# High weights times both halves of the rows in one matmul, in the stages of 256 tokens of a 6-layer transformer

## The reference

```python
def first_block(x, ...):                # 256 tokens
    for i in range(2):                  # i = 0: dilated attention, i = 1: mLSTM
        h = h + mixer(rms_norm(h), w_in, w_out)
        h = h + swiglu(rms_norm(h), ffn_w_in[i], ffn_w_out[i])

def swiglu(xn, w_in, w_out):            # D_FF = 2816
    gu = xn @ w_in
    return (jax.nn.silu(gu[..., :D_FF]) * gu[..., D_FF:]) @ w_out

def second_block(x, c, ctx, ...):       # 256 tokens, and 256 of context up to the last layer
    for i in range(4):                  # neighbourhood attention, conformer, short conv, attention
        x = x + mod_l[:, 2] * y_l
        m_l = modulate(rmsnorm(x, norm2_g[i]), mod_l[:, 3], mod_l[:, 4])
        x = x + mod_l[:, 5] * sq_relu_mlp(m_l, mlp_w1[i], mlp_w2[i])
        # the same for ctx while a later layer needs it

def sq_relu_mlp(h, w1, w2):             # 1024 -> 4096 -> 1024
    return jnp.square(jax.nn.relu(h @ w1)) @ w2
```

## Time and profile before

| | us |
|---|---|
| median of 3 runs | 2985.64 |
| lowest, highest | 2983.21, 2987.95 |
| span of the profiled execution | 2983.2 |
| TensorE busy in it | 2888.3 (97%) |
| TensorE's weight loads busy | 2524.0 (85%) |
| VectorE busy | 2004.9 (67%) |
| ScalarE busy | 1202.5 (40%) |
| GpSimd busy | 349.9 (12%) |

### The profile page before, as it was taken

How to read it: one execution, slowest core, us unless ns; L and a number is a source line. 1 busy time by engine, 2 the same in 40 slices (tenths; PEclk the granted TensorE clock), 3 DMA queues, 4 the chain that set the end, 5 groups by cost and what they waited for, 6 DMA issues and landing times.

```text
span 2983.2 us, 43523 instructions
## 1 busy us (share of the span) xinstructions
PE 2888.3 (97%) x18080; PEld 2524.0 (85%) x18080; DVE 2004.9 (67%) x3284; ACT 1202.5 (40%) x1993; POOL 349.9 (12%) x542
## 2 busy tenths in 40 slices
PE   7999999989999999999999999999999999998998
PEld 7999998889997778888866888888888888877898
DVE  7776887668655557777745677777777777554665
ACT  5444544554444444223314533223243222443543
POOL 0000001000022220000131100011010000243000
PEclk9999999999999999999999999999999999999999
DMA  7544675347655424555473255553535555465453
GB/s 241 168 159 152 216 229 190 120 161 234 204 125 81 72 64 147 157 167 169 132 190 107 80 168 163 169 165 124 170 120 164 168 163 169 117 96 86 142 184 128
DMA packets 362277, 451.85 MB, mean 151 GB/s; under 512 B 12656, under 2 KB 332432, under 8 KB 362080
## 3 DMA queue, kind: packets, MB, share of 16 engines
q1 hardware_dynamic: 326976, 329.83, 34.1%
q0 software_dynamic: 34944, 118.65, 16.9%
q10 hardware_dynamic: 160, 0.59, 0.1%
HBM read 438.60 MB, written 1.05 MB: 147 GB/s over the span
## 4 chain that ended last, share of the span: by engine, by line
PE 79%; DVE 12%; ACT 5%; DMA 2%; issue 1%; POOL 1%; DVEq 0%; SPq 0%; ACTq 0%
PE ps L1352 23%; PE ps L1354 23%; PE ps L1353 23%; DVE lo L1932 4%; PE ps L1530 1%; ACT hi L1602 1%; PE ps L1373 1%; PE ps L1517 1%; DVE NB L1963 1%; DMA NB<-in_na_rpb 1%; PE ps L1375 1%; PE ps L1374 1%; DVE MX L2008 1%; PE ps L1505 1%; DVE XN L1969 1%
## 5 line engine op out<-in xcount | busy, mean ns | idle before, releaser
L1352 PE MATMUL ps<-XN,hi 128*128 128x256 f32 (+1 forms) x3184 | 1048.8, 329 | 32.9 <-DVE XN L1949 9.9
L1353 PE MATMUL ps<-XN,hi 128*128 128x256 f32 (+1 forms) x3184 | 1029.9, 323 | 0.0
L1354 PE MATMUL ps<-XN,lo 128*128 128x256 f32 (+1 forms) x3184 | 1029.6, 323 | 0.0
L1932 DVE TENSOR_TENSOR lo<-raw,hi 128x1024 fp32r<-128x1024 f32 (+1 forms) x626 | 739.2, 1221 | 250.6 <-ACT hi L1602 245.4
L1602 ACT ACTIVATE hi<-raw 128x1024 fp32r<-128x1024 f32 (+1 forms) x626 | 620.6, 1040 | 443.5 <-PE ps L1354 440.7
L1352 PEld LDWEIGHTS ps<-XN,hi 128*128 128x128 f32 x3184 | 610.6, 192 | 106.6 <-issue 17.4
L1354 PEld LDWEIGHTS ps<-XN,lo 128*128 128x128 f32 x3184 | 610.8, 192 | 46.1
L1353 PEld LDWEIGHTS ps<-XN,hi 128*128 128x128 f32 x3184 | 611.2, 192 | 44.8
L2008 DVE CUSTOM_DVE_ANT_0 MX<-MW,C 128x1024 bf16<-128x1024 f32 x384 | 477.2, 1243 | 130.7 <-DMA MW<-in_mod_w 123.8
L1352 PE MATMUL ps<-H,hi 128*128 128x512 f32 (+1 forms) x1072 | 380.2, 355 | 0.0
L1353 PE MATMUL ps<-H,hi 128*128 128x512 f32 (+1 forms) x1072 | 379.7, 354 | 0.0
(11 more groups left out here) (255 smaller groups left out, 3194.8 us busy)
## 6 DMA issues: line engine op xcount, KB each, us to landing
raw<-in_mlp_w SPq DMA_DIRECT2D x128, 1024.0 KB, 5.3
MW<-in_mod_w POOLq DMA_DIRECT2D x192, 512.0 KB, 3.8
raw<-in_ffn_w_in SPq DMA_DIRECT2D x44, 1024.0 KB, 5.4
raw<-in_attn_w_in SPq DMA_DIRECT2D x36, 1024.0 KB, 4.9
raw<-in_na_wqkv SPq DMA_DIRECT2D x24, 1024.0 KB, 5.0
raw<-in_ffn_w_out SPq DMA_DIRECT2D x16, 1024.0 KB, 5.1
raw<-in_mlstm_w_in SPq DMA_DIRECT2D x12, 1024.0 KB, 5.1
raw<-in_cv_w SPq DMA_DIRECT2D x12, 1024.0 KB, 6.2
```

What stands on the lines that cost most here:

```text
L1352: e.matmul(out, whi, xhi, start=first, stop=False)
L1353: e.matmul(out, whi, xlo, start=False, stop=False)
L1354: i = e.matmul(out, wlo, xhi, start=False, stop=last)
L1932: e.tensor_tensor(lo[:, a:b], raw[:, a:b], hi[:, a:b].bitcast(F32), ALU.subtract).then_inc(*low.says(("lo", j, i), ("spent", j) if i else ...
```

## The change

A stage of 256 tokens fills half of a bank of 512 columns. With `pair`, one matmul of 512 columns takes the high weights against both halves of the rows: the hi half goes to columns 0 to 255, the lo half to 256 to 511. The matmul of the low weights against the high half adds to columns 0 to 255. The result is the sum of both halves of the bank, and the reader forms it. Pairing is on in attention q and k, the output projections of attention, mLSTM and the last layer, feed-forward down, and the last MLP. Feed-forward up, v projections, and everything of 512 tokens stay.

```diff
@@ TensorE
-    def product(j, t, k, kt, bank, x, first, last, whole=True, final=True):
+    def product(j, t, k, kt, bank, x, first, last, whole=True, final=True, pair=False):
...
-        e.matmul(out, whi, xhi, start=first, stop=False)
-        e.matmul(out, whi, xlo, start=False, stop=False)
-        i = e.matmul(out, wlo, xhi, start=False, stop=last)
+        if pair:
+            e.matmul(m.ps[b][:, :].rearrange("p (h n) -> p h n", h=2), whi, both_of(m, x, k), start=first, stop=False,
+                     skip_group_check=True)
+        else:
+            e.matmul(out, whi, xhi, start=first, stop=False)
+            e.matmul(out, whi, xlo, start=False, stop=False)
+        i = e.matmul(out, wlo, xhi, start=False, stop=last, skip_group_check=pair)
@@ new
+def both_of(m, x, k):
+
+    name = x[0]
+    if name in ("xn", "mo"):
+        return m.XN[:, :, k, x[2]:x[3]]
+    if name == "hf":
+        return m.HF[:, :, x[2] + k, :]
+    if name == "ob":
+        return m.OB[:, :, k, 0:x[3]]
+    return m.H2[:, x[2] % 2, :, k, 0:x[3]]
@@ ScalarE, dil_qk
-        e.activation(m.QK[:, pair % 2, g, which, t, :], m.ps[b][:, 0:S], ACT.Copy).then_inc(
-            *act.says(("free", b, u), ("qk", pair, g, which, t)))
+        e.activation(m.QK[:, pair % 2, g, which, t, :], m.ps[b][:, S:512], ACT.Copy).then_inc(
+            *act.says(("qk_low", pair, g, which, t)))
@@ ScalarE, mlp_up
-        e.activation(rl, m.ps[b][:, 0:n], ACT.Relu).then_inc(*act.says(("relu", layer, r)))
+        if n > S:
+            e.activation(rl, m.ps[b][:, 0:n], ACT.Relu).then_inc(*act.says(("relu", layer, r)))
+        else:
+            e.activation(m.RL[:, r % 4, S:512], m.ps[b][:, S:512], ACT.Copy).then_inc(*act.says(("uplow", layer, r)))
@@ VectorE, residual
+        if pair:
+            w.wait_ge(("acc", b, u), None if gate is None else ("mod", *gate))
+            for i in range(2):
+                part, x = m.ps[b][:, i * S:(i + 1) * S], m.X[:, j, 0:S]
+                if gate is None:
+                    f = e.tensor_tensor(x, part, x, ALU.add)
+                else:
+                    f = e.scalar_tensor_tensor(out=x, in0=part, scalar=mod_of(m, gate, j, 0), in1=x, op0=ALU.mult,
+                                               op1=ALU.add)
+                f.then_inc(*dve.says(*((("free", b, u), *names) if i else (("added", b, u),))))
+                w.wait_ge(None if i else ("added", b, u))
+            return
@@ VectorE, new
+    def dil_qk(pair, g, which, t, b, u):
+        dst = m.QK[:, pair % 2, g, which, t, :]
+        w.wait_ge(("qk_low", pair, g, which, t))
+        e.tensor_tensor(dst, m.ps[b][:, 0:S], dst, ALU.add).then_inc(
+            *dve.says(("free", b, u), ("qk", pair, g, which, t)))
@@ VectorE, mlp_up
+        else:
+            w.wait_ge(("uplow", layer, r))
+            e.tensor_tensor(both, m.ps[b][:, 0:S], both, ALU.add).then_inc(
+                *dve.says(("free", b, u), ("upsum", layer, r)))
+            w.wait_ge(("upsum", layer, r))
+            e.scalar_tensor_tensor(out=rl, in0=both, scalar=0.0, in1=both, op0=ALU.max, op1=ALU.mult).then_inc(
+                *dve.says(("relusq", layer, r)))
```

More of the change, by code:

```diff
@@ L361, in reads, with linear @@
             self.xn_used = [("used", j), ("used", j)]
-    def linear(self, w, layer, k0, kt, c0, cols, x, evac, adv=1, outer=False, until=None, quiet=False, hold=False, streams=None):
+    def linear(self, w, layer, k0, kt, c0, cols, x, evac, adv=1, outer=False, until=None, quiet=False, hold=False, streams=None, pair=False):
         j = self.take(w, layer, k0, kt, c0, cols)
@@ L383, in linear @@
                 for i, t in enumerate(group):
-                    self.do("product", j, t, k, kt, banks[i], x, k == 0, k == kt - 1)
+                    self.do("product", j, t, k, kt, banks[i], x, k == 0, k == kt - 1, True, True, pair)
                 if k < kt - 1:
@@ L541, in residual @@
             self.conditions_for(*gate)
-        self.do("residual", self.norms, j, n, gate, b, u, last)
+        self.do("residual", self.norms, j, n, gate, b, u, last, b is not None and n == S)
         if last:
@@ L565, in products @@
             for t in range(2):
-                self.do("product", units[c], t, k, KT, banks[c][t], x, k == 0, k == KT - 1)
+                self.do("product", units[c], t, k, KT, banks[c][t], x, k == 0, k == KT - 1, True, True, n == S)
         self.advance(2)
@@ L601, in grow @@
             self.linear(w, layer, 0, KT, c * 256, 256, x, evac, adv=adv if first else 1, outer=bool(first),
-                        until=first, quiet=c == 3, hold=c == 2 and n == 512)
+                        until=first, quiet=c == 3, hold=c == 2 and n == 512, pair=n == S)
             if first:
@@ L649, in queries_keys @@
             first = pair + g + which == 0
-            p.linear("attn_w_in", 0, 0, KT, ((g * 3 + which) * 8 + pair * 2) * P, 256, x, evac, outer=first)
+            p.linear("attn_w_in", 0, 0, KT, ((g * 3 + which) * 8 + pair * 2) * P, 256, x, evac, outer=first,
+                     pair=True)
             if first:
@@ L705, in swiglu @@
                     kk = k0 + k
-                    p.do("product", j, t, k, kt, banks[t], ("hf", layer, k0), kk == 0, kk == 21)
+                    p.do("product", j, t, k, kt, banks[t], ("hf", layer, k0), kk == 0, kk == 21, True, True, True)
                 if c < 3:
@@ L1154, in up @@
             p.linear("mlp_w1_2", layer, 0, KT, q * D + c * 256, 256, x, evac, outer=q + c == 0,
-                     streams=(0, 1) if q + c == 0 and n == 512 else None)
+                     streams=(0, 1) if q + c == 0 and n == 512 else None, pair=n == S)
     def down(q):
@@ L1165, in down @@
                 p.linear("mlp_w2_2", layer, q * D, KT, c * 256, 256, ("h2", layer, q, n), evac,
-                         quiet=q == 3 and c == 3, hold=(q, c, n) == (3, 2, 512))
+                         quiet=q == 3 and c == 3, hold=(q, c, n) == (3, 2, 512), pair=n == S)
     up(0)
@@ L1982, in residual_part, with residual @@
             *dve.says(("x", s, j, i), ("cv_res", j, i) if b is None else ("free", b, u)))
-    def residual(s, j, n, gate, b, u, last):
+    def residual(s, j, n, gate, b, u, last, pair=False):
         names = [("x", s, j)] if last else []
+        if pair:
[10 more added lines that the diff above has]
+            return
         if b is None:
@@ L2332, in mlp_up @@
     def mlp_up(layer, q, k, n, r, b, u):
-        rl = m.RL[:, r % 4, 0:n]
-        w.wait_ge(("relu", layer, r))
-        e.tensor_tensor(rl, m.ps[b][:, 0:n], rl, ALU.mult).then_inc(*dve.says(("free", b, u), ("relusq", layer, r)))
+        rl, both = m.RL[:, r % 4, 0:n], m.RL[:, r % 4, S:512]
+        if n > S:
+            w.wait_ge(("relu", layer, r))
+            e.tensor_tensor(rl, m.ps[b][:, 0:n], rl, ALU.mult).then_inc(
+                *dve.says(("free", b, u), ("relusq", layer, r)))
+        else:
[5 more added lines that the diff above has]
+                *dve.says(("relusq", layer, r)))
         w.wait_ge(("h2hi", layer, r))
@@ L2348, in vector @@
         "scale_part": scale_part, "rest_part": rest_part, "residual_part": residual_part,
-        "condition": condition, "mod_close": mod_close, "conditions": conditions, "dil_rotate": dil_rotate, "dil_scores": dil_scores,
+        "condition": condition, "mod_close": mod_close, "conditions": conditions, "dil_qk": dil_qk, "dil_rotate": dil_rotate, "dil_scores": dil_scores,
         "dil_turn": dil_turn, "dil_mix": dil_mix, "ffn_up": ffn_up, "ml_gates": ml_gates, "ml_columns": ml_columns,
```

## The result

The changed kernel takes 2999.12 us (median of 4 runs, 2994.07 to 3000.1) against 2985.52 for the kernel before on the same chip (4 runs): a ratio of 1.0047, with a 95% interval of 1.0035 to 1.0059. That is +13.6 us. Both lie inside the range, above the +3.4 that was forecast, and on the side of slower. One of e2's four executions (3555.22 us, at a mean granted clock of 0.75) was slow and is in no figure here.

The account below looks back on a forecast made before the run. TensorE, 98 to 100% busy, was taken as the bound, with VectorE not far behind. Last MLP +4, attention +2, projections +1.5 and downs -3.8 summed to +3.7 us: 2989 us from a median of 2985.6, range 2979 to 3000.

Parts of the forecast that it names:

- forecast (a): Whole kernel: VectorE and ScalarE take the saving back; 2984 to 2994 us, chance 0.60.
- rival (c): Paired matmuls: reading two runs of 256 columns costs the fixed part again, nothing saved; +14 us, 3000; chance 0.10.
- Last MLP, +4: Last MLP: up units' VectorE and ScalarE loop grows to 6.51 us against TensorE's 5.55; stage 4 us longer.
- The saving of 13.3 ns a product: All 1440 paired products: one fixed matmul part less each, 360.0 to 346.7 ns; 19.2 us if all on the path.
- Feed-forward down, layer 0, -1.9: Feed-forward downs: VectorE's 33% idle hides the first seven tiles' additions; 1.9 us shorter each, -3.8 together.
- Last projection, +0.5: Output projections, each: lo later by the previous tile's second addition, +0.9, less 0.4 saved by the units before.
- Attention, +2: Attention q and k: losses of 5.8 us against savings of 3.8, net +2; bounds -5.1 and +17.
- losses of 5.8 us: Attention: added VectorE additions delay heads and lo's; 5.8 us lost in all.
- 18 q and k units which TensorE paces: Attention: these units save 0.213 us each, 3.8 us in all.
- the 8 that were to be the sign of a wrong working: Attention: waits for lo adding up to over 8 us would show the prediction wrong.
- (b): Attention's idle time takes the additions and the last MLP's up loop overlaps; -7.4 us, 2978; chance 0.12.
- (d): Attention: the backlog spreads, half of the additions land on the path; +9 in place of +2, 2996; chance 0.18.

Follow-up runs that it names:

- e2: Changed kernel with three 256-column matmuls again, the low-half one to columns 256 to 511; readers' additions kept; 3006.2 us, ratio 1.0078.
- e1: Changed kernel with all pairs, but readers of the kernel before, reading columns 0 to 255 alone, no added additions; 2970.76 us, ratio 0.9962.
- e5: Changed kernel with the readers of both tiles of a unit interleaved in the last MLP's up units, same work; 2989.22 us, ratio 1.0019.
- e6: Changed kernel with the second tile's residual put behind the next unit's split in the feed-forward downs; 2993.89 us, ratio 1.0037.
- e4: Changed kernel without pairing in attention's q and k; 2993.28 us, ratio 1.0035.
- e8: Kernel before with pairs only in the feed-forward downs and the last MLP's down; 2984.27 us, ratio 1.0001.
- e9: Changed kernel, attention and projections as before; downs' second-tile readers behind the split, last MLP's up readers of both tiles together; 2979.05 us, ratio 0.9982.
- e7: Changed kernel with the two matmuls of every odd k turned round, narrow first; 2994.99 us, ratio 1.004.
- e11: Pairs with the readers of the kernel before, no added additions, and every odd k's two matmuls turned round; 2970.7 us, ratio 0.9951.
- e10: Changed kernel, pairs everywhere, with both order edits: downs' second-tile readers behind the split, last MLP's up readers interleaved; 2984.98 us, ratio 1.0001.

## Why the prediction was right or wrong

**Direction.** It gave slower 0.44 and no measurable difference 0.46; it was slower, by 10 to 14 us where 3.4 was the forecast. All that was missed points the same way. The 2999.12 lies outside forecast (a), 2984 to 2994, and inside the range only because that reached up to rival (c), whose mechanism did not show; that is luck. The forecast's mechanism, VectorE and ScalarE take back more than the matmuls save, is what the runs show (e1, e2, e5, e6).

**Last MLP, +4: right.** Measured +4.2 and +4.1. Inside it two smaller errors cancel. The loop is 6.38 us and not 6.51: the second operation reads no PSUM, and takes 0.42, where the 477 ns of the earlier trace rows was used. The waits of TensorE are 0.5 us each, half of what was forecast. Against that TensorE's own saving is smaller, by the rhythm (481 pairs at 351.5 ns, some 2.3 us lost). That the loop is the cause is shown by e5, which takes it away without taking any work away.

**The saving of 13.3 ns a product: right in one rhythm, too large in the other.** The sum took 346.7 ns for every pair. The runs have 346.7 in some stretches and 353.3 in others. For 1440 products the mean of 9.2 ns makes 13.2 us in place of 19.2. The sign that it named, the matmul behind a wide one starting 227 ns after it, came out as another spacing, 230 or 237; in the faster rhythm the step behind the narrow one, 116.7 and not 120, makes the sum right all the same.

**Feed-forward down, layer 0, -1.9: wrong, +2.0.** The step that failed is "VectorE's 33% idle hides the first seven tiles' additions". VectorE had the time, but the additions stand between the tile's end and ScalarE's square, and the next hi stands behind that square. The reserve of that chain counts, not the engine's idle share; e6, which changes that order alone, makes it -0.4. The waits for lo account for 2.4 us of the 3.9 between forecast and measurement, and the rhythm (351.7 ns a pair in that stage) for 0.9. In layer 1's down, -1.9 was right (-2.2): there the same additions cost 0.0 (e2). The layer-0 stage has modulation products on VectorE (L2040, four instructions from 449.68) ahead of these additions; that they take the reserve there is argued, not shown.

**Last projection, +0.5: mis-sized, +2.2 to +3.6.** The step had the right mechanism ("lo is later by the previous tile's second addition") at the price of one addition. It left out that `grow_wide` reads four tiles at once (3.73 us in one burst), that the gated additions take 0.48 each and need each other, and that lo to lo then takes 5.68 us, over TensorE's 5.55. The backlog never falls before the end, and the norm's sum comes 2.7 us later after TensorE's last product (3.0 against 0.34). How much of the row is that and how much the clock of the single profile (see the result) cannot be said closer than 2.2 to 3.6. The attention's projection with its plain additions has 5.45 us from lo to lo (291.56 to 297.01), and e4 shows no cost for it.

**Attention, +2: mis-sized, +3.8 to +5.6.** The losses of 5.8 us were near (e2, which saves nothing, has +6.2). The savings were not: of "18 q and k units which TensorE paces" at 0.213 each, the rhythm leaves 350 to 351 ns a pair, 2.7 us instead of 3.8. What remains of the difference is within what a single profile can tell. The waits for lo grew by 4.5 us, under the 8 that were to be the sign of a wrong working.

**The rivals.** (b) is out: the last MLP's loop does not overlap by itself. (c) is out as put: pairs at 346.7 ns read the same two runs of columns, so there the pair has its full saving. Its time, 3000, is near the measured one for another reason. Its +3.4 for attention does not follow from the prediction's own terms either: with nothing saved, the losses of 5.8 would stand (e2: +6.2). Whether reading in two runs has a part in the 353.3 was not tried. (d) is out in its size: attention is not at +9.

**What stays open.** What picks the rhythm. It holds until the series of pairs is broken and can be the other one after that; the same tiles show both (`HF` in both downs), and the stage does not decide (the last MLP is at 346.7 in e1 and at 353.3 in e5, e8 and e9). The order of widths decides that there are two at all (e7, e11 have one), but not which of them a stretch gets. Nor is it known why a wide matmul's step is 230.0 ns at its shortest here, or what the step would be with both halves of the rows side by side.

Ten runs of e1 fall into two groups, seven at 2968.9 to 2971.5 us and three at 2977.5 to 2979.7. The distance of 8 us would fit 1440 pairs at 6.6 ns (9.5), but only one of the runs has a profile. The clock is a rival: the three have a mean granted clock of 0.989 to 0.991, the seven 0.991 to 0.994. A difference of 0.002 over 2970 us is up to 6 us of TensorE's time. e8 shows the same, six runs up to 2984.6 us at 0.990 to 0.993 and four from 2987.2 us on at 0.989 or 0.990. No run here parts the two causes.

## What to carry to other kernels

Work moved from TensorE to an engine that reads its results must be placed in the chain from the tile's last matmul to the next weight split, on both engines, and compared with the time of a unit; an engine's idle share does not say whether it fits. The cure is in the order, not in the amount: read two tiles in step, or put the split ahead of a reader that has time. Use such a pairing stage by stage, where TensorE sets the pace and the readers have reserve; here three stages of it, with both changes of order, gain 5.9 us (e9); all of it as first written loses 10 to 14, and all of it with both changes of order is even (e10). Before a difference of a few microseconds in a stage is read from two single profiles, compare the granted clocks of that stage.

## What the runs showed of the hardware

Alternating matmuls of 512 and 256 columns, each with its own weights, run at 346.7 ns a pair (230.0 behind the wide one, 116.7 behind the narrow) or at 353.3 (236.7 and 116.7) at the same granted clock of 1.00, and keep the one that they have until they are broken off. With the order turned in every other pair there is one rhythm, 348.3 ns a pair in the long series. The kernel before, with equal widths in a stage, shows 120.0 and 226.7 ns alone. Pairs that read 512 columns as two runs of 256 can run at 346.7 ns, the sum of 120.0 and 226.7; whether the two runs have a part in the 353.3 is not shown. On VectorE two additions that need each other take 0.88 us for the pair, plain, and 0.96 gated (1.91 for four). In every trace the granted clock falls to 0.50 (1.2 GHz) for some microseconds, 11 to 15 times; over the last projection of the kernel before it is 0.87 on the mean, over the matmuls of the downs 1.00.
